# Two-block transformer on one core: the modulation weights with their outputs on partitions, multiplied by VectorE and summed by ScalarE, where TensorE summed them

## The chip, the cores and the metric

One core of one Trainium2 chip runs the whole program. The metric is the device time of one execution in microseconds (us), here the median of three runs.

## The reference

A token array of 512 x 1024 (and later a context of 256 x 1024) goes through two blocks of a first kind (feed-forward, a mixer, feed-forward) and two of a second kind (attention and an MLP). All arithmetic is fp32. Ahead of each of the ten sub-layers stands a modulation: a vector `c` of 1024 numbers is put through silu and multiplied by a 1024 x 3072 matrix, which gives shift, scale and gate for 1024 channels each.

```python
def modulate(x, shift, scale):
    return x * (1.0 + scale) + shift

c_act = jax.nn.silu(c)
for l in range(DEPTH):
    mod = (c_act @ ada_w[l] + ada_b[l]).reshape(b, N_SUB, 3, 1, D_MODEL)
    h = modulate(x, mod[:, 0, 0], mod[:, 0, 1])
    y = swiglu_ffn(h, ffn1_w_in[l], ffn1_w_out[l])
    x = layer_norm(ALPHA * x + 0.5 * mod[:, 0, 2] * y, ln_g[l, 0], ln_b[l, 0])
    ...
```

In the second kind of block there are two such vectors for each matrix, `c_2` for the tokens and `c_ctx_2` for the context. The matrices are numbered m = 0 to 9: m below 6 has one vector, m from 6 on has two. It is this product, vector times matrix, that the change computes in another way. The large matrix products are not touched.

## The kernel before

**The large products.** Each linear layer (`Linear`) is cut into units of weights of up to 128 x 2048. SyncE loads a unit into one of two slots of `raw` (`load_unit`, L893), ScalarE rounds it into `w_hi` (`round_weights`, L1263), VectorE subtracts to get the remainder `w_lo` (`split_weights`, L2760), and TensorE multiplies three times per 128 rows (`passes`, L1935 to L1937): low weights with high data, high with low, high with high. Units alternate between two slots, so unit i is rounded once unit i-2 has been used. In a layer "gateup" (`ffn..._in`) a unit is two tiles of eight chunks, 48 matmuls of 512 columns; ScalarE applies silu to the gate tile (L1299), VectorE multiplies by the other (`val_t`, L2808), ScalarE rounds the result (`hid_hi`, L1305), VectorE takes the remainder (`hid_lo`, L2814). A layer `ffn..._out` has 8 units of one tile each with 12 or 10 chunks. In the MLPs of the second kind of block both streams run: 16 x 3 matmuls of 512 and as many of 256 columns for a unit; ScalarE applies relu (L1340) to each tile.

**The modulation.** Each matrix is cut into 12 units of 128 x 2048 (2 groups of 128 output channels, 8 chunks of 128 inputs; inputs lie on partitions). The first 5 units (`DIRECT`) of m = 0 are multiplied by TensorE, the next 3 (`EARLY`) and all others are spread over the gateup units, one per unit, from the first layer on: 64 units of one vector up to `ffn1_in_1_0`, then 24 units with two vectors in `ffn1_in_1_1`, `ffn2_in_1_0` and the first two units of `ffn2_in_1_1`, then 24 with two vectors over the MLP of the first second-kind block (`number`, `Seg`). Two further slots of `raw` hold these units (`load_ada`, L887). VectorE multiplies a unit by `c` (a number per partition) and adds over the eight chunks: one tensor_scalar and seven scalar_tensor_tensor of 128 x 256 for each vector (`ada_unit`, L2843 and L2846), each waiting for the one before. TensorE then sums the 128 partitions by a matmul with a column of ones:

```python
for q in range(2):
    for v in range(nv):
        mm = eng.matmul(ps[:, B_ADA, at(48 * m + v + (i * 2 + q) * nv)], ada_acc[:, b, v, q * P:(q + 1) * P],
                        ones[:, 0:1], start=True, stop=True, skip_group_check=True)
mm.then_inc(s_asum, 1)
```

**What sets the order.** The order is written out by hand per engine. TensorE's `linear` calls `ada_sums` (L1929) for unit i-2 behind the matmuls of unit i. VectorE's `linear` does, per unit, the remainder of the weights, the evacuation of unit i-2, the modulation unit i-2. ScalarE rounds unit i and evacuates unit i-2. SyncE loads unit i of the layer and modulation unit i-1, the latter once unit i-3 has been multiplied (`s_ada`). `finish` closes a layer: for its last two units it rounds and splits the first two of the following layer, evacuates and, on VectorE, does the modulation unit. At the end, `vectors_of` (before each norm) reads all sums of a matrix.

Of the kernel before, what the change touches and what calls it, by code (L numbers as in the profile page):

```python
# [67 lines left out]
class Seg:  # L68


    def __init__(self, lo, hi, m, u0, a0, p0):
        self.lo, self.hi, self.m, self.u0, self.a0, self.p0 = lo, hi, m, u0, a0, p0
# [81 lines left out]
def ada_parts(m):  # L154

    return DC * vectors(m) - 1


def number(sched):
# [3 lines left out]
    parts = len(EARLY) * ada_parts(0)  # L163
# [29 lines left out]
    for item in sched:  # L193
        if item[0] in ("norm", "ctx_in"):
            item[1].asum = ada
            assert item[1].m is None or m > item[1].m, item[1].name
        if item[0] == "lin":
# [3 lines left out]
            while lo < ln.n and m < 10 and (ln.evac == "gateup" or ln.name == "ffn1_out_0_0" if m < 8 else  # L201
                                            ln.name.startswith("mlp")):
                hi = min(ln.n, lo + ADA_UNITS - u0)
                ln.ada.append(Seg(lo, hi, m, u0, ada, parts))
                u0, ada, parts = u0 + hi - lo, ada + hi - lo, parts + (hi - lo) * ada_parts(m)
# [3 lines left out]
            ln.asum = ada  # L209
# [70 lines left out]
def build(nc, t_in, out):  # L280
# [4 lines left out]
    with ExitStack() as ctx:  # L285
        arena_bytes = 212800
        arena = ctx.enter_context(nc.sbuf_tensor("arena", [P, arena_bytes // 4], F32))
        base = 16512
# [44 lines left out]
        kept = place("kept", [P, 2 * MOD], F32, arena_bytes - 8 * MOD)  # L333
# [12 lines left out]
        assert after("ada_acc") <= used["kept"][0] and after("relu_t") <= after("val_t")  # L346
# [33 lines left out]
        a_head = place("a_head", [P, SSD_H], F32, after("logf"))  # L380
        cacc = place("cacc", [P, 4, SEQ], F32, used["raw"][0] + 2 * 4 * SLOT)
# [186 lines left out]
        s_part = sem("ada_partial_products")  # L568
        s_ada = sem("ada_unit_used")
        s_asum = sem("ada_unit_summed")  # L570
        s_keep = sem("ada_sums_kept")
# [190 lines left out]
        KEPT = {"gqa": 7, "mla": 9}  # L762
# [111 lines left out]
        def _(eng):  # L874
# [22 lines left out]
            for j, item in enumerate(sched):  # L897
                if item[0] == "start":
# [93 lines left out]
        def _(eng):  # L992
# [244 lines left out]
        def _(eng):  # L1237
# [96 lines left out]

            def rectified(ln, i, pos, q):
# [2634 lines left out]
```

## Time and profile before

| | us |
|---|---|
| median of 3 runs (3991.22 to 3994.91) | 3994.83 |
| the profiled execution | 3987.11 |
| its span on the chip | 3985.3 |
| TensorE busy | 3856.9 (97%) |
| VectorE busy | 2538.5 (64%) |
| ScalarE busy | 1385.0 (35%) |
| mean granted TensorE clock | 0.983 of full speed |

PE is TensorE's matmuls, PEld its weight loads (they run beside the matmuls), DVE is VectorE, ACT ScalarE, POOL GpSimd, SP SyncE. A line number is that of the kernel before. A timeline row gives start, duration, engine, line, operation, what is written and read, and how often; in brackets stands how long the engine had been idle and who released it. The profiled execution's time and its span lie 1.8 us apart.

### The profile page before, as it was taken

The numbers are of one execution on the slowest core, as the hardware profiler recorded it, in microseconds if no ns is written. First come the engines' busy times: TensorE is split into PE (matmuls) and PEld (weight loads), VectorE is DVE, ScalarE is ACT, GpSimd is POOL, SyncE is SP. The second block draws the span as 40 slices with busy tenths as digits, with TensorE's granted clock in tenths as the row PEclk, the third lists the DMA queues.
The fourth block names the chain that finished last, engine by engine and source line by source line (L and its number), as shares of the span: only waits on it lengthen the run. The fifth ranks groups of instructions, "written<-read, shape, count | busy, mean of one in ns | idle before, by whom it ended". The sixth has DMA issues, their size and how long they took to land.

```text
span 3985.3 us, 52107 instructions
## 1 busy us (share of the span) xinstructions
PE 3856.9 (97%) x20570; PEld 3256.3 (82%) x20570; DVE 2538.5 (64%) x4095; ACT 1385.0 (35%) x1994; POOL 562.0 (14%) x559
## 2 busy tenths in 40 slices
PE   8999999999999999999998989899999999999998
PEld 6888877888888888788887678888888887888886
DVE  5666776755674677778445489686665367866335
ACT  2222334322232224432222168531221235853223
POOL 1000402200120012130004200150000152113001
PEclk8999999999999999999999989999999999999999
DMA  4554212344343432125322011213322112322221
GB/s 193 192 210 160 84 64 74 138 147 169 138 151 134 178 108 75 43 99 197 127 80 86 11 26 31 74 63 127 127 106 106 59 48 63 70 78 85 95 95 64
DMA packets 71231, 416.00 MB, mean 104 GB/s; under 512 B 8928, under 2 KB 12128, under 8 KB 30048
## 3 DMA queue, kind: packets, MB, share of 16 engines
q1 hardware_dynamic: 69744, 406.63, 29.0%
q10 hardware_dynamic: 1264, 6.29, 0.4%
q8 instruction: 153, 2.51, 0.3%
q14 instruction: 70, 0.57, 0.0%
HBM read 391.92 MB, written 2.10 MB: 99 GB/s over the span
## 4 chain that ended last, share of the span: by engine, by line
PE 82%; DVE 13%; ACT 2%; issue 2%; POOL 2%; DMA 0%; DVEq 0%; ACTq 0%; POOLq 0%
PE ps L1935 25%; PE ps L1936 24%; PE ps L1937 24%; DVE nmax L3726 2%; PE ps L1929 1%; PE ps L2654 1%; DVE w_lo L2760 1%; POOL sq_h_lat L1057 1%; DVE gp_lo L3743 1%; DVE x_lat L3086 1%; DVE rstd_lat L3075 1%; DVE mp_lo L3743 1%; DVE gprob L3738 1%; DVE x_lat L3097 1%; PE ps L2183 1%
## 5 line engine op out<-in xcount | busy, mean ns | idle before, releaser
L1935 PE MATMUL ps<-h_hi,w_lo 128*128 128x512 f32 (+2 forms) x2872 | 1089.9, 379 | 39.8 <-DVE h_lo L3105 17.9
L1937 PE MATMUL ps<-h_hi,w_hi 128*128 128x512 f32 (+2 forms) x2872 | 1069.3, 372 | 0.0
L1936 PE MATMUL ps<-h_lo,w_hi 128*128 128x512 f32 (+1 forms) x2800 | 1043.2, 373 | 0.0
L1263 ACT ACTIVATE w_hi<-raw 128x2048 fp32r<-128x2048 f32 (+3 forms) x262 | 457.8, 1748 | 1368.6 <-PE ps L1937 1326.0
L2760 DVE TENSOR_TENSOR w_lo<-raw,w_hi 128x2048 fp32r<-128x2048 f32 (+3 forms) x262 | 557.9, 2130 | 575.8 <-ACT w_hi L1263 575.5
L1935 PEld LDWEIGHTS ps<-h_hi,w_lo 128*128 128x128 f32 (+1 forms) x2872 | 545.3, 190 | 145.4 <-DVE h_lo L3105 22.5
L1937 PEld LDWEIGHTS ps<-h_hi,w_hi 128*128 128x128 f32 (+1 forms) x2872 | 545.1, 190 | 95.9
L1936 PEld LDWEIGHTS ps<-h_lo,w_hi 128*128 128x128 f32 x2800 | 531.8, 190 | 86.7 <-issue 0.5
L2846 DVE SCALAR_TENSOR_TENSOR ada_acc<-raw,c_act,ada_acc 128x256 f32<-128x256 f32 x1141 | 499.9, 482 | 16.8
L1935 PE MATMUL ps<-hid_hi,w_lo 128*128 128x512 f32 (+1 forms) x1272 | 499.2, 392 | 8.6 <-DVE w_lo L2760 6.5
L1937 PE MATMUL ps<-hid_hi,w_hi 128*128 128x512 f32 (+1 forms) x1272 | 490.4, 386 | 0.0
L1936 PE MATMUL ps<-hid_lo,w_hi 128*128 128x512 f32 (+1 forms) x1272 | 490.2, 385 | 0.0
L1935 PEld LDWEIGHTS ps<-hid_hi,w_lo 128*128 128x128 f32 x1272 | 240.2, 189 | 62.7 <-DVE w_lo L2760 8.8
L1937 PEld LDWEIGHTS ps<-hid_hi,w_hi 128*128 128x128 f32 x1272 | 240.0, 189 | 51.9
L1936 PEld LDWEIGHTS ps<-hid_lo,w_hi 128*128 128x128 f32 x1272 | 240.3, 189 | 50.4 <-issue 1.2
L1028 POOL TENSOR_TENSOR x_sum_lat<-x_lat 128x512 f32<-128x512 f32 x10 | 14.1, 1411 | 1866.6 <-DVE x_lat L3152 1319.8
L3152 DVE SCALAR_TENSOR_TENSOR x_lat<-ps,mod_lat,x_lat 128x512 f32<-128x512 f32 x70 | 52.5, 750 | 183.9 <-PE ps L1937 178.1
L1057 POOL TENSOR_SCALAR sq_h_lat<-x_lat,mod_lat 128x256 f32<-128x256 f32 x144 | 133.6, 935 | 168.3 <-DVE x_lat L3097 168.3
L3726 DVE TENSOR_REDUCE nmax<-ps 128x1 f32<-128x768 f32 x160 | 134.7, 843 | 7.5 <-PE ps L1937 5.6
L1305 ACT ACTIVATE hid_hi<-val_t 128x512 f32 (+1 forms) x88 | 55.6, 632 | 224.7 <-DVE val_t L2808 224.7
L1935 PE MATMUL ps<-hc_hi,w_lo 128*128 128x256 f32 x424 | 122.3, 289 | 8.3 <-DVE hc_lo L3105 8.3
L1441 ACT ACTIVATE h_hi<-x_lat,mod_lat 128x256 fp32r<-128x256 f32 x144 | 79.8, 595 | 125.6 <-DVE x_lat L3097 125.6
(488 smaller groups left out, 6054.1 us busy)
## 6 DMA issues: line engine op xcount, KB each, us to landing
raw<-ada SPq DMA_DIRECT2D x114, 1024.0 KB, 4.9
raw<-ffn_in SPq DMA_DIRECT2D x87, 1024.0 KB, 6.7
raw<-mlp_in SPq DMA_DIRECT2D x32, 1024.0 KB, 4.9
raw<-mlp_out SPq DMA_DIRECT2D x32, 1024.0 KB, 5.1
raw<-ffn_out SPq DMA_DIRECT2D x32, 768.0 KB, 5.4
raw<-ffn_out SPq DMA_DIRECT2D x32, 640.0 KB, 4.0
raw<-mix_p SPq DMA_DIRECT2D x14, 1024.0 KB, 4.8
raw<-mix_x SPq DMA_DIRECT2D x8, 1024.0 KB, 4.9
```

Source lines behind the costliest of these rows:

```text
L1057: eng.tensor_scalar(h32[:, k, part.cs], x[:, k, part.cs], g[:, k:k + 1], b[:, k:k + 1], ALU.mult, ALU.add).then_inc(s_n32, 1)
L1263: eng.activation(w_hi[:, slot, 0:ln.width], raw[:, slot, 0:ln.width], ACT.Copy).then_inc(s_whi, 1)
L1305: eng.activation(hid_hi[:, at(i), :], val_t[:, pos % 2, 0:SEQ].unsqueeze(1), ACT.Copy)\
L1441: eng.activation(hi[:, k, part.cs], x[:, k, part.cs], ACT.Identity, bias=b[:, k:k + 1], scale=g[:, k:k + 1]).then_inc(s_nhi, 1)
L1935: eng.matmul(out, lo_w, hi_x, start=first, stop=False, skip_group_check=True)
L1936: eng.matmul(out, hi_w, lo_x, start=False, stop=False, skip_group_check=True)
L1937: return eng.matmul(out, hi_w, hi_x, start=False, stop=last, skip_group_check=True)
L2760: eng.tensor_tensor(w_lo[:, slot, 0:ln.width], raw[:, slot, 0:ln.width], w_hi[:, slot, 0:ln.width].bitcast(F32), ALU.subtract).then_inc(s_ ...
L2846: ins = eng.scalar_tensor_tensor(acc, weights[:, :, k, :], c_act[:, c:c + 1], acc, ALU.mult, ALU.add)
L3152: a = eng.scalar_tensor_tensor(x, ps[:, tile_bank(ln, m, st), 0:NT[st]], MODT[st][:, ln.gate[st], 2 * DC + m:2 * DC + m + 1], x, ALU.mult, ...
L3726: eng.reduce_max(nmax[:, k % 8:k % 8 + 1], flat(2 * (k % 2))[:, 0:nk], AX_X, negate=True).then_inc(t_mx, 1)
L3743: eng.tensor_tensor(a.p[1][:, k % NPT, :], ps[:, B_PT + k % 2, :], a.p[0][:, k % NPT, :].bitcast(F32), ALU.subtract).then_inc(t_pl, 1)
```

## The change

The modulation weights of all but the first eight units are laid out the other way round: a partition now holds one output channel with its 1024 inputs in a row. VectorE multiplies a whole unit (128 x 2048) by the activated vector, which is laid out along the row and is the same on all partitions (`c_row`, two tensors of 1024 numbers): one tensor_tensor per vector in place of eight instructions. ScalarE runs a Copy over each half of the product (128 x 1024) with its accumulating output, which gives the sum of a row: two activations per vector. TensorE keeps the sums of the three `EARLY` units only, with VectorE's old code for them (`early_unit`, `early_sums`).

Where a product goes:

```diff
+        def product_of(seg, pos, v):
+            if in_place(seg.m, v):
+                return raw[:, 2 + (seg.a0 - seg.lo + pos) % 2, :]
+            if seg.m >= 8:
+                return products2[:, :]
+            return products[:, (seg.s0 + (pos - seg.lo) * vectors(seg.m) + v) % 2, :]
```

On SyncE's queue: the rows of `c`, and a further wait for m = 8 and 9.

```diff
+                    eng.dma_start(c_row[:, 0, :], t_in["c_rows"][0, :].partition_broadcast(P)).then_inc(s_crow, 16)
...
                             eng.wait_ge(s_ada, i + (seg.a0 - seg.lo - 1))
+                            if seg.m >= 8:
+                                eng.wait_ge(s_asum, i * 2 + (seg.s0 - 2 * seg.lo - 2))
...
+                            if ln is rows_ln and i == 4:
+                                eng.wait_ge(s_ada, first_pair.a0)
+                                for v in range(2):
+                                    eng.dma_start(c_row[:, v, :], t_in["c_rows"][1 + v, :].partition_broadcast(P))\
+                                       .then_inc(s_crow, 16)
```

On ScalarE: the sums, one unit behind the evacuation, and at a layer's end.

```diff
+            def ada_sums(seg, i, pos):
+                if seg:
+                    nv, u = vectors(seg.m), seg.u0 - seg.lo
+                    for v in range(nv):
+                        if v + 1 < nv:
+                            eng.wait_ge(s_prod, i + (seg.a0 - seg.lo - first_pair.a0 + 1))
+                        else:
+                            eng.wait_ge(s_ada, i + (seg.a0 - seg.lo + 1))
+                        for q in range(2):
+                            p = product_of(seg, pos, v)[:, q * D:(q + 1) * D]
+                            a = eng.activation(p, p, ACT.Copy, accum_out=sums_of(seg.m)[:, at(i * 2 * nv + (2 * u + q) * nv + v)])
+                        a.then_inc(s_asum, 1)
...
                         round_weights(ln, i, it, lo + u)
                         evacuate(ln, i - 2, it, lo + u - 2)
+                        ada_sums(seg, i - 3, lo + u - 3)
                 finish(ln, lag, following)
...
                     if not first:
                         evacuate(ln, i, 0, i)
+                    if i:
+                        ada_sums_of(ln, i - 1)
                 if following:
                     ahead(following, lag, 2)
+                ada_sums_of(ln, ln.n - 1)
```

On TensorE: the call for the sums goes.

```diff
-                            main(lo + u, i)
-                            if ln.g0 == 0 and lo + u == 7:
-                                eng.wait_ge(s_late, 1)
-                            ada(seg, lo + u - 2, i - 2)
+                    for it, u, i in steps(eng, done, ln.n):
+                        main(done + u, i)
```

On VectorE: a product for each vector.

```diff
+            def ada(seg, i, it, pos):
+                if seg:
+                    nv, n = vectors(seg.m), seg.a0 - seg.lo + pos
+                    raw_ready(eng, 2 + n % 2, n, it)
+                    weights = raw[:, 2 + n % 2, :].rearrange("p (q k) -> p q k", q=2)
+                    eng.wait_ge(s_silu, nv)
                     for v in range(nv):
+                        if not in_place(seg.m, v) and seg.s0 + (pos - seg.lo) * nv + v >= 2:
+                            eng.wait_ge(s_asum, i * nv + (seg.s0 - seg.lo * nv + v - 1))
+                        ins = eng.tensor_tensor(product_of(seg, pos, v).rearrange("p (q k) -> p q k", q=2), weights,
+                                                c_row[:, v, :].unsqueeze(1).broadcast_to([P, 2, D]), ALU.mult)
+                        ins.then_inc(s_prod if v + 1 < nv else s_ada, 1)
```

A product has its own place: two buffers of 128 x 2048 in the space of the context for m below 8, one (`products2`) for the first vector and the slot of `raw` itself for the second (`in_place`) for m = 8 and 9. So VectorE waits, before it writes a product buffer, until ScalarE has summed what was in it, and SyncE, for m = 8 and 9, until the product in the slot is summed. ScalarE activates the rows of `c` itself (`c_rows`: once in the first layer, once at the end of `ffn1_out_1_0`). The sums lie in SBUF (`ada_sum`, `kept`) and no longer in a PSUM bank, so the two copies `keep` and the waits for them go. To find the room the region for DMA descriptors is cut from 16 to 8 KiB per partition.

TensorE's queue in a gateup layer (names: `h_hi`, `h_lo` the data, `w_hi`, `w_lo` the weights, `ada_acc` the partial sums). Before, at a unit's end:

```order
L1936 MATMUL ps<-h_lo,w_hi 128x512
L1937 MATMUL ps<-h_hi,w_hi 128x512
L1929 MATMUL ps<-ones,ada_acc 128x1 x2
L1935 MATMUL ps<-h_hi,w_lo 128x512
L1936 MATMUL ps<-h_lo,w_hi 128x512
```

After the change the two matmuls on `ada_acc` are gone and nothing stands in their place.

ScalarE's queue at the end of `ffn1_in_1_1`, the layer with two vectors per unit, where `ffn1_out_1_1` (units of 128 x 1280) begins. Before:

```order
L1263 ACTIVATE w_hi<-raw 128x1280
L1299 ACTIVATE gate_t<-ps 128x512
L1305 ACTIVATE hid_hi<-val_t 128x512
L1263 ACTIVATE w_hi<-raw 128x1280
L1299 ACTIVATE gate_t<-ps 128x512
L1305 ACTIVATE hid_hi<-val_t 128x512
L1263 ACTIVATE w_hi<-raw 128x1280 x5
```

After the change:

```order
L1296 ACTIVATE w_hi<-raw 128x1280
L1332 ACTIVATE gate_t<-ps 128x512
L1338 ACTIVATE hid_hi<-val_t 128x512
L1379 ACTIVATE products,ada_sum<-products 128x1024 x4
L1296 ACTIVATE w_hi<-raw 128x1280
L1332 ACTIVATE gate_t<-ps 128x512
L1338 ACTIVATE hid_hi<-val_t 128x512
L1379 ACTIVATE products,ada_sum<-products 128x1024 x8
L1296 ACTIVATE w_hi<-raw 128x1280 x5
```

Eight sums, those of the last two units, now stand ahead of the rounding of the third unit of the following layer (the first of the x5).

VectorE's queue at the same place. Before:

```order
L2760 TENSOR_TENSOR w_lo<-raw,w_hi 128x1280
L2808 TENSOR_TENSOR val_t<-ps,gate_t 128x512
L2814 TENSOR_TENSOR hid_lo<-val_t,hid_hi 128x512
L2843 TENSOR_SCALAR ada_acc<-raw,c_act 128x256 x2
L2846 SCALAR_TENSOR_TENSOR ada_acc<-raw,c_act,ada_acc 128x256 x14
L3152 SCALAR_TENSOR_TENSOR x_lat<-ps,mod_lat,x_lat 128x512
L2760 TENSOR_TENSOR w_lo<-raw,w_hi 128x1280
```

After the change:

```order
L2803 TENSOR_TENSOR w_lo<-raw,w_hi 128x1280
L2851 TENSOR_TENSOR val_t<-ps,gate_t 128x512
L2857 TENSOR_TENSOR hid_lo<-val_t,hid_hi 128x512
L2899 TENSOR_TENSOR products<-raw,c_row 128x2048 x2
L3196 SCALAR_TENSOR_TENSOR x_lat<-ps,mod_lat,x_lat 128x512
L2803 TENSOR_TENSOR w_lo<-raw,w_hi 128x1280
```

Two products stand where sixteen small instructions stood; the rest has kept its place.

## Rows read from the trace of the kernel before

**Rows 1.** The page: busy time, shares of the chain, a transfer (us to landing last).
```profile
PE 3856.9 (97%) x20570; PEld 3256.3 (82%) x20570; DVE 2538.5 (64%) x4095; ACT 1385.0 (35%) x1994; POOL 562.0 (14%) x559
...
PE 82%; DVE 13%; ACT 2%; issue 2%; POOL 2%; DMA 0%; DVEq 0%; ACTq 0%; POOLq 0%
...
raw<-ffn_in SPq DMA_DIRECT2D x87, 1024.0 KB, 6.7
```

**Rows 2.** Groups by line and shape: busy us, mean ns of one | idle before.
```profile
L2760 DVE TENSOR_TENSOR w_lo<-raw,w_hi 128x2048 fp32r<-128x2048 f32 x187 | 431.4, 2308 | 408.5 <-ACT w_hi L1263 408.3
L1929 PE MATMUL ps<-ones,ada_acc 128*128 128x1 f32 x652 | 79.3, 236 | 0.0
L1411 ACT ACTIVATE sq_h_lat<-x_lat 128x1024 f32<-128x1024 f32 x18 | 19.1, 1061 | 19.3 <-DVE x_lat L3025 18.9
L1817 ACT ACTIVATION_READ_ACCUMULATOR gprob<-ps,nmax 128x1 f32 x96 | 18.7, 195 | 0.0
```

**Rows 3.** Timeline of ACT, rounding: one vector, two vectors, no modulation units.
```profile
118.76 1.92 ACT L1263 ACTIVATE w_hi<-raw 128x2048 fp32r<-128x2048 f32 x1 [5.84 <-PE ps L1937]
130.11 1.92 ACT L1263 ACTIVATE w_hi<-raw 128x2048 fp32r<-128x2048 f32 x1 [5.84 <-PE ps L1937]
...
1352.59 1.92 ACT L1263 ACTIVATE w_hi<-raw 128x2048 fp32r<-128x2048 f32 x1 [6.28 <-PE ps L1937]
1364.40 1.92 ACT L1263 ACTIVATE w_hi<-raw 128x2048 fp32r<-128x2048 f32 x1 [6.21 <-PE ps L1937]
...
2057.87 1.92 ACT L1263 ACTIVATE w_hi<-raw 128x2048 fp32r<-128x2048 f32 x1 [5.37 <-PE ps L1937]
2068.75 1.27 ACT L1263 ACTIVATE w_hi<-raw 128x1280 fp32r<-128x1280 f32 x1 [5.37 <-PE ps L1937]
```

**Rows 4.** Timeline of PE at a unit's end in the MLP with both streams.
```profile
3084.02 0.29 PE L1937 MATMUL ps<-hc_hi,w_hi 128*128 128x256 f32 x1
...
3084.95 0.48 PE L1935 MATMUL ps<-h_hi,w_lo 128*128 128x512 f32 x1
...
3085.50 0.39 PE L1937 MATMUL ps<-h_hi,w_hi 128*128 128x512 f32 x1
```

**Rows 5.** Timelines of DVE, PE and POOL at the beginning of `ffn2_in_1_0`.
```profile
1782.95 1.04 DVE L2814 TENSOR_TENSOR hid_lo<-val_t,hid_hi 128x512 fp32r<-128x512 f32 x1
1784.76 6.05 DVE L2846 SCALAR_TENSOR_TENSOR ada_acc<-raw,c_act,ada_acc 128x256 f32<-128x256 f32 x14
...
1793.76 0.47 PE L1935 MATMUL ps<-h_hi,w_lo 128*128 128x512 f32 x1 [0.97 <-DVE val_t L2808]
...
1774.53 12.45 POOL L1069 TENSOR_SCALAR x_lat<-x_lat,aff_lat 128x256 f32<-128x256 f32 x16
```

**Rows 6.** Timeline of ACT where an exponential with accumulating output is followed by another.
```profile
2324.84 0.90 ACT L1817 ACTIVATE gprob<-ps,nmax 128x768 f32<-128x768 f32 x1 [1.39 <-DVE nmax L3726]
...
2325.73 0.89 ACT L1817 ACTIVATE gprob<-ps,nmax 128x768 f32<-128x768 f32 x1
```

**Rows 7.** Timeline of ACT at the end of `ffn1_in_1_1` and of `ffn2_in_1_0`.
```profile
1423.31 1.27 ACT L1263 ACTIVATE w_hi<-raw 128x1280 fp32r<-128x1280 f32 x1 [7.74 <-PE ps L1937]
...
1426.74 0.63 ACT L1305 ACTIVATE hid_hi<-val_t 128x512 fp32r<-128x512 f32 x1 [1.67 <-DVE val_t L2808]
1431.17 1.27 ACT L1263 ACTIVATE w_hi<-raw 128x1280 fp32r<-128x1280 f32 x1 [3.80 <-PE ps L1937]
...
1899.34 1.49 ACT L1263 ACTIVATE w_hi<-raw 128x1536 fp32r<-128x1536 f32 x1 [7.26 <-PE ps L1937]
...
1903.25 0.63 ACT L1305 ACTIVATE hid_hi<-val_t 128x512 fp32r<-128x512 f32 x1 [1.94 <-DVE val_t L2808]
1908.61 1.49 ACT L1263 ACTIVATE w_hi<-raw 128x1536 fp32r<-128x1536 f32 x1 [4.72 <-PE ps L1937]
```

**Rows 8.** Timeline of ACT in an MLP unit with both streams and no modulation.
```profile
3111.17 0.87 ACT L1340 ACTIVATE relu_t<-ps 128x512 f32<-128x512 f32 x2 [5.74 <-PE ps L1937]
...
3127.89 0.87 ACT L1340 ACTIVATE relu_t<-ps 128x512 f32<-128x512 f32 x2 [4.86 <-PE ps L1937]
```

More of the change, by code:

```diff
@@ L151, in vectors, with in_place @@
     return 1 if m < 6 else 2
-def ada_parts(m):
-    return DC * vectors(m) - 1
+def in_place(m, v):
+    return m >= 8 and v == 1
 def number(sched):
@@ L162, in number @@
     ada = len(EARLY)
-    parts = len(EARLY) * ada_parts(0)
+    sums = 0
     m, u0 = 0, len(DIRECT) + len(EARLY)
@@ L332, in build @@
         hc_lo = place("hc_lo", [P, DC, CTX], F32R, after("hc_hi"))
-        kept = place("kept", [P, 2 * MOD], F32, arena_bytes - 8 * MOD)
+        c_row = place("c_row", [P, 2, D], F32, arena_bytes - 8 * D)
+        kept = place("kept", [P, 2 * MOD], F32, arena_bytes - 8 * D - 8 * MOD)
+        ada_sum = place("ada_sum", [P, 4, 2 * MOD], F32, used["kept"][0] - 32 * 32)
+        products = place("products", [P, 2, SLOT], F32, used["hc_hi"][0])
         A = after("hc_lo")
@@ L345, in build @@
         ada_acc = place("ada_acc", [P, 2, 2, 2 * P], F32, after("val_t"))
-        assert after("ada_acc") <= used["kept"][0] and after("relu_t") <= after("val_t")
+        products2 = place("products2", [P, SLOT], F32, after("relu_t"))
+        assert after("ada_acc") <= used["ada_sum"][0] and after("relu_t") <= after("val_t")
+        assert after("products2") <= used["ada_sum"][0] and after("products") <= A and after("ada_sum") <= used["kept"][0]
         sq_a = {"lat": place("sq_a_lat", [P, DC, SEQ], F32, A)}
@@ L864, in weight_half, with sums_of @@
             return slice(h * ln.width // 2, (h + 1) * ln.width // 2)
+        first_pair = next(seg for item in sched if item[0] == "lin" for seg in item[1].ada if vectors(seg.m) == 2)
+        rows_ln = next(item[1] for item in sched if item[0] == "lin" and any(seg is first_pair for seg in item[1].ada))
+        rows_ln = sched[next(j for j, item in enumerate(sched) if item[1] is rows_ln) - 1][1]
+        assert rows_ln.n == DC and not rows_ln.ada and not first_pair.lo and not first_pair.u0
+        def sums_of(m):
+            return kept[:, :] if m in (7, 9) else ada_sum[:, m % 4, :]
+        def product_of(seg, pos, v):
[4 more added lines that the diff above has]
+            return products[:, (seg.s0 + (pos - seg.lo) * vectors(seg.m) + v) % 2, :]
         def raw_ready(eng, slot, n, it):
@@ L1333, in evacuate, with ada_sums_of, c_rows @@
                         a.then_inc(s_hidhi, 1)
+            def ada_sums(seg, i, pos):
[10 more added lines that the diff above has]
+                        a.then_inc(s_asum, 1)
+            def ada_sums_of(ln, i):
+                for lo, hi, seg in runs(ln, 0, i, i + 1):
+                    ada_sums(seg, i, i)
+            def c_rows(n):
+                eng.wait_ge(s_crow, 16 if n == 0 else 48)
+                c = c_row[:, 0, :] if n == 0 else c_row[:, :, :]
+                eng.activation(c, c, ACT.Silu).then_inc(s_silu, 1)
             def rectified(ln, i, pos, q):
@@ L1375, in linear @@
                     third_unit(ln)
-                for lo, hi, _ in runs(ln, 2, lag + (ln.halved is not None), ln.n):
+                if ln.g0 == 0:
+                    c_rows(0)
+                for lo, hi, seg in runs(ln, 3, lag + (ln.halved is not None), ln.n):
                     for it, u, i in steps(eng, lo, hi):
@@ L2150, in linear @@
                     return
-                if before and before.ada:
-                    ada_of(before, before.n - 2)
-                    if ln.n > 1:
-                        main(1, 1)
-                        done = 2
-                    ada_of(before, before.n - 1)
                 if ln.norm:
@@ L3532, in mixer @@
                 w.h_chunks += DC
-            def keep(kind):
-                m = KEPT[kind]
-                eng.wait_ge(s_asum, ADA_UNITS * (m + 1) - len(DIRECT))
-                eng.tensor_copy(kept[:, :], ps[:, B_ADA, 48 * m:48 * m + 2 * MOD]).then_inc(s_keep, 1)
             def split_keys(v):
```

134 lines of the change are left out of this document (61 added, 73 removed).

## The prediction, made before the change was run

> **What bounds the kernel.** I read the page first: TensorE is busy 97% of the span, VectorE 64%, ScalarE 35%, and the chain of work that ended last lies on TensorE for 82% [rows 1]. So a microsecond of TensorE's queue is worth a microsecond of the whole, and one of VectorE or ScalarE nothing, as long as they hand their results over in time. Then I read the groups by line and shape for what the sums cost TensorE, and the timelines for how long a unit takes with and without them. The group [rows 2] has 652 records of L1929 (each fp32 matmul leaves two), 79.3 us in all; but matmuls overlap, so the time that they take from the queue is read from the distance of unit to unit. ScalarE rounds the next unit as soon as TensorE has ended one, which makes its rounding a clock for TensorE's progress: 130.11 - 118.76 = 11.35 us with one vector, 1364.40 - 1352.59 = 11.81 with two, 2068.75 - 2057.87 = 10.88 where no modulation unit is left [rows 3]. 10.88 is 48 matmuls at 0.227 with nothing between, so a unit's end costs nothing by itself and the sums are the whole difference.
>
> **TensorE: what goes.** With one vector 11.35 - 10.88 = 0.47 us per unit, 64 units: 30.1. With two vectors in the gateup layers 0.93, 24 units: 22.3. In the MLP with both streams I take TensorE's own rows: from the last matmul before the sums to the third after them 3085.50 - 3084.02 = 1.48 us [rows 4]. Without sums it would be one of 256 columns and two of 512; a unit there takes 3127.89 - 3111.17 = 16.72 for 48 of each [rows 8], so 0.12 for the one and 0.57 for the three. That leaves 0.91, 24 units: 21.8. Together **74.2 us**. The three EARLY units keep their sums. The waits and copies for the kept sums cost TensorE nothing I can see, and I take nothing for them.
>
> **VectorE: what goes.** A unit's eight or sixteen small instructions become one or two products of 128 x 2048 with both inputs in SBUF. The row nearest in shape and kind is the remainder of the weights, 2.31 us [rows 2], and I take 2.3. Two vectors: 4.6 in place of over 6 (14 of the 16 alone took 6.05 in [rows 5]). TensorE rarely waits for this: at the beginning of `ffn2_in_1_0` the sixteen stand ahead of the fourth unit's remainder, and TensorE idles 0.97 before it goes on [rows 5]. The products end over a microsecond sooner, so I count **1.0 us** gained. The next thing late there is ScalarE's rounding, which is long done. The remaining gain on VectorE is worth nothing: it lies beside TensorE's matmuls.
>
> At this place GpSimd runs until 1786.98 (12.45 from 1774.53), and VectorE's remainder took 1.04 there [rows 5], where other instructions of its kind take about 0.7. So a product that begins there is stretched, by my estimate 0.5 to 1 us over the pair, and it still ends in time. The Trainium skill speaks against the change here (SBUF — State Buffer, "Who interferes with whom"): a VectorE instruction with two SBUF inputs contends with a GpSimd instruction that reads SBUF, and whoever issues first holds the shared pair for its whole duration. Taken as a full block, the first product would wait out GpSimd's last 3 us, the 1.0 would not be gained, and the sum would come out about 1 us higher.
>
> **ScalarE: what comes.** 2 activations per vector and unit, 64 x 2 + 48 x 4 = 320, each with a read of the accumulator. A square of the same 128 x 1024 takes 1.06, the read 0.195 [rows 2]; one after the other without overlap 1.25. But in the row of exponentials the next one starts 2325.73 - 2324.84 = 0.89 after the one before, read included, though the activation alone lasts 0.90 [rows 6]: the read hides in the overlap. So I take **1.05 per sum**, with 1.25 as the upper end; the lower end of their cost to TensorE is nothing. That is 336 us more on ScalarE, 1385 to about 1720, 43% of the span.
>
> Do they hide? In a gateup unit with one vector ScalarE gets 2.1 us more in 10.88, behind its evacuation. With two vectors there is a ring: VectorE may write a product only when ScalarE has summed the one before in that buffer. That ring is: four sums 4.2, the last product 2.3, then the remainder, `val_t` and `hid_hi` before ScalarE can sum again: the rounding to the end of `hid_hi` is 1427.37 - 1423.31 = 4.06 with narrow weights [rows 7], of which 1.27 is the rounding; the remainder of the full width adds 0.9, so 3.7. The ring is 10.2, under 10.88 (with 1.25 per sum 11.0, level with it). And TensorE needs the split weights only at the end of the unit, 10.88 - 1.92 - 2.31 = 6.7 us after they are there. SyncE's load of the next gateup unit stands behind its wait for the product, which ends some 1.5 us into the following unit; landing takes 6.7 [rows 1], before the 10.88 are over. In the MLP a unit's first product ends about 8.4 us after its odd tile (relu 0.87, rounding 1.92, remainder 2.31, the hidden tile's remainder about 1, product 2.3), the four sums at 12.6; the relu of the next tile, due at 8.4, must be through with its square by 16.7 [rows 8]: 12.6 + 0.9 + 1.0 = 14.5, so it hides.
>
> They don't hide at a layer's end. There eight sums stand ahead of the third rounding of the following layer. In `ffn1_out_1_1`, with the rounding at 1423.31 as zero: `hid_hi` ends at 4.06, the sums of the last unit but one at 8.3; the last unit's products, each waiting for a buffer, end at 8.5 and 10.8, their sums at 10.6 and 12.9; rounding 1.27 gives 14.2, the remainder (1280 of 2048 columns of 2.31, 1.4) 15.6. TensorE has done two units of 1431.17 - 1423.31 - 0.93 = 6.93, 13.9 [rows 7]: **1.7 us lost**. The same for `ffn2_out_1_0`: `hid_hi` at 4.54, sums at 13.4, rounded 14.9, split 16.6, against 2 x (9.27 - 0.93) = 16.7: nothing. With 1.25 per sum the two lose 2.9 and 1.1, 4.0. With one vector four sums end before 10, and nothing is lost.
>
> Edits with no cost: the first row of `c` (512 KB) is loaded while TensorE is at the opening's own sums, its silu (about 1.1 us of ScalarE, by the square's row) stands ahead of the fourth rounding, on a queue that is idle most of the time there; the other two rows load and activate in `ffn1_out_1_0`, where no modulation unit is due. If that cover were gone it would be 1 to 2 us each, once. The smaller descriptor region I cost at nothing: its price shows in no row.
>
> **The sum.** -74.2 - 1.0 + 1.7 = **-73.5 us**. The profiled execution, 3987.1 (span 3985.3 and 1.8 around it), becomes 3913.6. The median of the runs lies 7.7 above the profiled execution; I take the same difference from it: 3994.8 - 73.5 = **3921**.
>
> **Rivals.**
> (a) *ScalarE's sums are dearer, 1.3 to 1.6 us, and the ring fills.* At 1.5: the ring is 12.0, 1.1 over for 24 units, of which the 6.7 of slack in each of three stretches swallow all but some 6; the two ends lose 5.3 and 3.5. Loss 15 in place of 1.7: 3934. For it: the upper bound of 1.25 is near, and sums written through a register address show in no row. Against: the overlap of [rows 6].
> (b) *The accumulating Copy costs twice a plain one, and ScalarE's ring becomes the bound.* It decides from about 1.9 us per sum: the ring is 13.6, 2.7 over, 65 less 20 of slack is 45; in the 12 `mlp_in` units the relu comes 4 x 1.9 - 6.3 = 1.3 late, 16; the ends lose 8 x 0.85 more each, 15: 76, all that was gained. At 2.12 (two squares) it is 65 + 26 + 19 = 110, 35 more than is gained: 4030. For it: one ring holds both engines and the product's buffers. Against: the exponentials with accumulator cost no more than their width.
> (c) *The change doesn't free TensorE*: something else fills the places of the sums, time 3995. Against: [rows 3], where units without sums follow at full rate.
>
> **How the numbers follow.** Forecast 0.80; (a) 0.11; (b) 0.05; (c) 0.04. 0.2% of the time is 8 us, about what runs can tell from no change. Faster by more: 0.91; within it 0.04; slower 0.05. Range: low end 3910, where no sum is paid for, other short waits for VectorE shrink with its load, and the runs' own scatter of 4 us is added; high end 3940, which takes in 1.25 per sum and all of (a).
>
> **What would show it.** Right: ScalarE's roundings 10.88 apart in all gateup stages; TensorE's 652 records on `ada_acc` down to 12; ScalarE near 1720 us busy, VectorE some 170 us less; 320 sums 1.05 apart; one new wait of TensorE of 1 to 3 us near the beginning of `ffn1_out_1_1`. Wrong: periods over 10.88 with two vectors and ScalarE never idle in them (a, b); idle TensorE at each unit's end (c); waits of ScalarE for transfers that reach TensorE.

## The result, and the profile after

The changed kernel takes **3922.8 us** (median of 4 runs, 3916.2 to 3930.5) against 3993.0 (4 runs, 3989.6 to 3994.9) of the kernel before: 70.2 us less, ratio 0.983 with a 95% interval of 0.982 to 0.985. The forecast was 3921, and 73.5 less. The profiled execution is the longest of the four, 3930.5 (span 3928.7, granted clock 0.980), so its distance to the profiled execution of before, 56.7, is not the gain; where most of the other 14 us went is told below.

Line numbers are now those of the changed kernel: rounding L1296, split L2803, sum L1379, product L2899, the three passes L2000 to L2002, a hidden chunk's split L2857 and L2968, evacuation into `x_lat` L2870 and L3196. First its page:

```profile
PE 3793.1 (97%) x19930; PEld 3189.2 (81%) x19930; DVE 2365.4 (60%) x2973; ACT 1724.5 (44%) x2636; POOL 575.9 (15%) x559
```

Against [rows 1], TensorE has 640 records fewer (12 of the 652 are left), VectorE is 173 us less busy, ScalarE 340 more. The groups by line and shape give the prices of the new instructions:

```profile
L2899 DVE TENSOR_TENSOR products<-raw,c_row 128x2048 f32<-128x2048 f32 x136 | 309.3, 2289 | 27.7 <-ACT products L1379 27.7
L1379 ACT ACTIVATE products<-products 128x1024 f32<-128x1024 f32 x272 | 284.2, 1048 | 119.3 <-DVE products L2899 119.3
L1379 ACT ACTIVATION_READ_ACCUMULATOR products<-products 128x1 f32 x240 | 44.2, 184 | 0.0
```

A product takes 2.29 us, a sum 1.05, its read 0.18. In the timeline of ScalarE, a one-vector stretch and a two-vector unit, the answer to [rows 3]:

```profile
126.00 1.92 ACT L1296 ACTIVATE w_hi<-raw 128x2048 fp32r<-128x2048 f32 x1 [3.29 <-PE ps L2002]
136.88 1.92 ACT L1296 ACTIVATE w_hi<-raw 128x2048 fp32r<-128x2048 f32 x1 [3.29 <-PE ps L2002]
...
1331.22 1.92 ACT L1296 ACTIVATE w_hi<-raw 128x2048 fp32r<-128x2048 f32 x1 [1.21 <-PE ps L2002]
1336.63 1.04 ACT L1379 ACTIVATE products<-products 128x1024 f32<-128x1024 f32 x1
1337.67 1.05 ACT L1379 ACTIVATE products<-products 128x1024 f32<-128x1024 f32 x1
...
1342.10 1.92 ACT L1296 ACTIVATE w_hi<-raw 128x2048 fp32r<-128x2048 f32 x1 [1.21 <-PE ps L2002]
```

The roundings stand 10.88 apart with one vector and with two; sums follow each other in 1.04 (the read hides, as in [rows 6]); and ahead of each rounding ScalarE is still idle for 1.21 with two vectors. VectorE too waits for that rounding:

```profile
1344.05 2.29 DVE L2803 TENSOR_TENSOR w_lo<-raw,w_hi 128x2048 fp32r<-128x2048 f32 x1 [0.72 <-ACT w_hi L1296]
```

So the ring, which runs over VectorE's products, could close 0.72 us sooner than it does: it is not full. The waits of TensorE by releaser, of the kernel after:

```profile
PE ps L2000 <- DVE w_lo L2803: 17.9, 8, 5.9
...
PE ps L2000 <- DVE hidc_lo L2968: 4.5, 4, 1.1
...
PE ps L2000 <- DVE x_lat L2870: 0.8, 1, 0.8
```

and of the kernel before:

```profile
PE ps L1935 <- DVE w_lo L2760: 16.0, 6, 5.9
...
PE ps L1935 <- DVE hidc_lo L2922: 1.9, 4, 1.1
PE ps L1935 <- DVE val_t L2808: 1.0, 1, 1.0
```

The wait of 1.0 for `val_t` is gone [rows 5]. New are 1.9 more for `w_lo` (1.8 of it at one place), 0.8 for `x_lat` at one place, and 2.6 more for the hidden chunks at three. The first is the end of `ffn1_in_1_1`, here in the timelines of ScalarE, VectorE and TensorE:

```profile
1396.50 1.28 ACT L1296 ACTIVATE w_hi<-raw 128x1280 fp32r<-128x1280 f32 x1 [2.65 <-PE ps L2002]
...
1400.47 1.05 ACT L1379 ACTIVATE products<-products 128x1024 f32<-128x1024 f32 x1
...
1408.36 1.04 ACT L1379 ACTIVATE products<-products 128x1024 f32<-128x1024 f32 x1
1409.40 2.42 ACT L1296 ACTIVATE w_hi<-raw 128x1280 fp32r<-128x1280 f32 x2
...
1410.68 1.49 DVE L2803 TENSOR_TENSOR w_lo<-raw,w_hi 128x1280 fp32r<-128x1280 f32 x1 [2.76 <-ACT w_hi L1296]
...
1410.06 0.40 PE L2002 MATMUL ps<-hid_hi,w_hi 128*128 128x512 f32 x1
1412.23 0.50 PE L2000 MATMUL ps<-hid_hi,w_lo 128*128 128x512 f32 x1 [1.77 <-DVE w_lo L2803]
```

With the rounding at 1396.50 as zero, the eight sums end and the third rounding begins at 12.9, and the split is done at 15.7: the forecast's numbers to 0.1. From matmul to matmul TensorE takes 2.17 in place of 0.23, so **1.95 us** are lost. The second is the end of `ffn2_in_1_0`, VectorE and TensorE:

```profile
1879.19 1.76 DVE L2803 TENSOR_TENSOR w_lo<-raw,w_hi 128x1536 fp32r<-128x1536 f32 x1 [3.73 <-ACT w_hi L1296]
1880.87 0.74 DVE L2870 SCALAR_TENSOR_TENSOR x_lat<-ps,mod_lat,x_lat 128x512 f32<-128x512 f32 x1
...
1880.57 0.40 PE L2002 MATMUL ps<-hid_hi,w_hi 128*128 128x512 f32 x1
1881.76 0.47 PE L2000 MATMUL ps<-hid_hi,w_lo 128*128 128x512 f32 x1 [0.80 <-DVE x_lat L2870]
```

The split is there with the last matmul of the second unit, as forecast, but TensorE waits for the bank of the first tile, and its evacuation stands *behind* the split on VectorE: **0.97 us** lost. The third place is the handover from `mlp_in` to `mlp_out`, on TensorE, which comes four times:

```profile
2810.89 0.40 PE L2002 MATMUL ps<-hid_hi,w_hi 128*128 128x512 f32 x1
2812.42 0.51 PE L2000 MATMUL ps<-hid_hi,w_lo 128*128 128x512 f32 x1 [1.13 <-DVE hidc_lo L2968]
```

Here it takes 1.53 in place of 0.23, 1.30 lost at each. Before, it was 0.44 at three of the four, and 1.30 at the last, where no modulation unit was due any more:

```profile
2716.52 0.40 PE L1937 MATMUL ps<-hid_hi,w_hi 128*128 128x512 f32 x1
2717.18 0.50 PE L1935 MATMUL ps<-hid_hi,w_lo 128*128 128x512 f32 x1 [0.26 <-DVE hidc_lo L2922]
```

The tally: -74.2 - 1.0 + 1.95 + 0.97 + 3 x 0.87 = **-69.7**, against -70.2 between the medians. That they agree to half a microsecond is luck, for the interval of the ratio is 11 us wide. And the traces give the sums a little less than 74.2. Both have the same 19918 records of matmuls besides the sums' own, so each can be laid beside its counterpart ("aligned" here and below). Over the places of the sums the changed kernel gains 29.6, 21.9 and 21.3 us, together 72.8: a unit with two vectors gave 0.92 in a gateup layer but 0.88 at an output layer and in the MLP.

**The profiled execution's missing 14 us.** Aligned with it, the changed kernel is 7.7 us behind before at 106 us (8.3 at 80), and the work there is the same. The windows of the opening show why, first the kernel before, then the kernel after:

```profile
0.00:50.00 50.00, 44.25 (x198) 34.95 (x199) 26.07 (x33) 12.96 (x13) 6.22 (x21) 0.80 0.71 282
50.00:100.00 50.00, 41.86 (x173) 34.07 (x172) 24.54 (x52) 13.13 (x15) 10.10 (x13) 0.89 0.27 102
```
```profile
0.00:50.00 50.00, 44.31 (x174) 33.49 (x174) 26.06 (x33) 12.91 (x13) 6.22 (x21) 0.75 0.66 269
50.00:100.00 50.00, 41.87 (x159) 34.50 (x160) 17.81 (x35) 12.20 (x14) 10.10 (x13) 0.78 0.25 89
```

The number ahead of the last two is the granted clock: 0.80 and 0.89 against 0.75 and 0.78. The trace holds 30.7 us at the lower level (1.2 GHz) before 100 us in the one, 47.8 in the other. The experiments' profiles show that this goes with the run and not with the change. From 106 us on the two profiles differ by 64.4, some 4 less than the terms add up to (72.8 + 1.0 less the 5.5 of the three places): 1.5 are a stretch of 3.4 us at the lower level at 1666.4 us, which the other profiles don't have there, and the rest, between 2100 and 3600 us, I did not follow.

### The profile page after: what moved, and what is told of

It reads as the page before. It is cut to its first block, busy times and chain, and to the rows that moved or that the text cites. A ratio compares the mean times of both kernels' runs of the same rounds, so it can differ in the third digit from the quotient of the medians.

```text
span 3928.7 us, 49772 instructions
## 1 busy us (share of the span) xinstructions
PE 3793.1 (97%) x19930; PEld 3189.2 (81%) x19930; DVE 2365.4 (60%) x2973; ACT 1724.5 (44%) x2636; POOL 575.9 (15%) x559
## 4 chain that ended last, share of the span: by engine, by line
PE 81%; DVE 13%; ACT 2%; issue 2%; POOL 2%; DMA 0%; DVEq 0%; ACTq 0%; POOLq 0%
PE ps L2000 25%; PE ps L2001 24%; PE ps L2002 24%; DVE nmax L3762 2%; DVE w_lo L2803 1%; PE ps L2697 1%; DVE gp_lo L3779 1%; POOL sq_h_lat L1090 1%; DVE x_lat L3130 1%; DVE rstd_lat L3119 1%; PE ps L2228 1%; DVE mp_lo L3779 1%; DVE gprob L3774 1%; DVE x_lat L3141 1%; DVE h_lo L3149 1%
## 5 line engine op out<-in xcount | busy, mean ns | idle before, releaser
L2000 PE MATMUL ps<-h_hi,w_lo 128*128 128x512 f32 (+2 forms) x2872 | 1085.7, 378 | 40.9 <-DVE h_lo L3149 19.4
L2002 PE MATMUL ps<-h_hi,w_hi 128*128 128x512 f32 (+2 forms) x2872 | 1071.1, 373 | 0.0
L2803 DVE TENSOR_TENSOR w_lo<-raw,w_hi 128x2048 fp32r<-128x2048 f32 (+3 forms) x262 | 558.2, 2131 | 657.6 <-ACT w_hi L1296 657.3
L1296 ACT ACTIVATE w_hi<-raw 128x2048 fp32r<-128x2048 f32 (+3 forms) x262 | 457.6, 1747 | 972.3 <-PE ps L2002 961.5
L2000 PEld LDWEIGHTS ps<-h_hi,w_lo 128*128 128x128 f32 (+1 forms) x2872 | 546.7, 190 | 148.5 <-DVE h_lo L3149 23.3
L2002 PEld LDWEIGHTS ps<-h_hi,w_hi 128*128 128x128 f32 (+1 forms) x2872 | 546.6, 190 | 95.3
L2000 PE MATMUL ps<-hid_hi,w_lo 128*128 128x512 f32 (+1 forms) x1272 | 496.3, 390 | 13.8 <-DVE w_lo L2803 8.5
L2002 PE MATMUL ps<-hid_hi,w_hi 128*128 128x512 f32 (+1 forms) x1272 | 490.4, 386 | 0.0
L1379 ACT ACTIVATE products<-products 128x1024 f32<-128x1024 f32 x272 | 284.2, 1048 | 119.3 <-DVE products L2899 119.3
L2899 DVE TENSOR_TENSOR products<-raw,c_row 128x2048 f32<-128x2048 f32 x136 | 309.3, 2289 | 27.7 <-ACT products L1379 27.7
L2000 PEld LDWEIGHTS ps<-hid_hi,w_lo 128*128 128x128 f32 x1272 | 239.7, 188 | 70.5 <-DVE w_lo L2803 12.3
L2002 PEld LDWEIGHTS ps<-hid_hi,w_hi 128*128 128x128 f32 x1272 | 239.7, 188 | 52.4
L3196 DVE SCALAR_TENSOR_TENSOR x_lat<-ps,mod_lat,x_lat 128x512 f32<-128x512 f32 x70 | 52.4, 749 | 177.3 <-PE ps L2002 171.4
L1338 ACT ACTIVATE hid_hi<-val_t 128x512 fp32r<-128x512 f32 (+1 forms) x88 | 55.6, 632 | 212.1 <-DVE val_t L2851 212.1
```

What stands on the lines that cost most here:

```text
L1296: eng.activation(w_hi[:, slot, 0:ln.width], raw[:, slot, 0:ln.width], ACT.Copy).then_inc(s_whi, 1)
L1338: eng.activation(hid_hi[:, at(i), :], val_t[:, pos % 2, 0:SEQ].unsqueeze(1), ACT.Copy)\
L1379: a = eng.activation(p, p, ACT.Copy, accum_out=sums_of(seg.m)[:, at(i * 2 * nv + (2 * u + q) * nv + v)])
L2000: eng.matmul(out, lo_w, hi_x, start=first, stop=False, skip_group_check=True)
L2002: return eng.matmul(out, hi_w, hi_x, start=False, stop=last, skip_group_check=True)
L2803: eng.tensor_tensor(w_lo[:, slot, 0:ln.width], raw[:, slot, 0:ln.width], w_hi[:, slot, 0:ln.width].bitcast(F32), ALU.subtract).then_inc(s_ ...
```

## The experiments

The first four ran beside 15 runs of the kernel before (median 3995.6), the last three beside 15 more (3995.1), all on one chip. Run 1 is the changed kernel, against which the others are read.

**1. The change again.** No edit.

> The changed kernel once more, unaltered, as the measure for the three runs beside it. Expected: 69 to 71 us under the kernel before (0.982 to 0.983 of it). Its first four runs lay between 3916 and 3930 us with granted clocks of 0.983 to 0.980, so single runs should again differ by some 10 us and go with the granted clock; if the profiled run has a clock of 0.983, its opening should be as long as the opening before. If instead the opening of the changed kernel is slower in itself (its matmul groups of 16 at 7 us against 9.6 us in the two profiles), some 8 us should be lost in the first 80 us in this profile too.

3925.0 (3918.7 to 3930.0, 5 runs), ratio 0.982 (0.981 to 0.984): 70.5 us less. The profiled run lost 3.9 us in the opening, with 41.0 us at the lower level. Both new waits are at their places with the same 1.95 and 0.97. Directly behind the first, which ends at 1408.7 here, the clock falls for 3.4 us (from 1410.0), which the first profile did not have.

**2. ScalarE's last sums behind the rounding.**

```diff
+                if ln.ada and following and following.n > 2 and len(following.streams) == 1:
+                    w.held = ln
+                else:
+                    ada_sums_of(ln, ln.n - 1)
...
                     round_weights(ln, i, 0, i)
+                    held_sums()
...
+                    if ln.evac == "resid" and ln.n > 2 and ln.halved is None:
+                        evacuate(ln, done - 2, 0, done - 2)
+                        split_weights(ln, done, 0, done)
```

> The changed kernel with two edits at the end of a layer: ScalarE takes the sums of the layer's last unit behind the third rounding of the layer that follows (not ahead of it), and in the output layers without a norm VectorE evacuates the first tile ahead of the third split. My reading of the trace after (new waits of 1.95 us near 1410 and 0.97 us near 1881 on TensorE) says that both waits go and nothing takes their place: 2.9 us under the changed kernel. The rival reading, that these waits belong to a late transfer or a bank and not to the eight sums, leaves both where they are: 0. Total difference is below the scatter of single runs, so the two places in the trace decide.

3920.1 (3916.5 to 3925.3, 5 runs), 0.982 (0.981 to 0.983), 4.9 under run 1, within its scatter. The places decide. ScalarE's timeline, with four sums where there were eight:

```profile
1388.67 1.28 ACT L1298 ACTIVATE w_hi<-raw 128x1280 fp32r<-128x1280 f32 x1 [2.64 <-PE ps L2022]
1396.80 1.26 ACT L1298 ACTIVATE w_hi<-raw 128x1280 fp32r<-128x1280 f32 x1
1402.66 1.27 ACT L1298 ACTIVATE w_hi<-raw 128x1280 fp32r<-128x1280 f32 x1 [0.44 <-PE ps L2022]
```

The third rounding (1396.80) begins 8.1 us after the second in place of 12.9, TensorE's waits for `w_lo` are back to 16.2, and the one for `x_lat` L2870 is gone. Aligned with run 1, the kernel gains 3.6 us at the first place (1.95, and the rest is the 3.4 us at half clock that followed it) and 1.0 at the second, and nothing is lost between. Both waits belong to the order on the two engines: the first to the sums ahead of the rounding, the second to the split ahead of the evacuation.

**3. TensorE's matmuls put back.**

```diff
+                def idle(seg):
+                    if seg:
+                        for j in range(2 * vectors(seg.m)):
+                            eng.matmul(ps[:, B_ADA, j:j + 1], ones[:, :], ones[:, 0:1], start=True, stop=True,
+                                       skip_group_check=True)
```

> The changed kernel, with ScalarE and VectorE as they are, but TensorE gets its fp32 matmuls of one column back at the old places: two per unit with one vector, four per unit with two, on constants, into an unused bank, and nobody waits for them. If TensorE's own time is the whole gain (64 x 0.47 + 24 x 0.93 + 24 x 0.91 = 74.2 us, of which some 2.6 us stand in the cover of the hidden chunks' last chain), the time goes back to the kernel before within 4 us: about 3990 to 3994 (0.999 to 1.000 of it). If part of the gain came from VectorE's lighter work or from waits between the engines, it stays under the kernel before by that part: 3960 to 3985.

3990.1 (3986.7 to 3996.3, 11 runs), 0.9994 (0.9985 to 1.0003). The gain is gone, as it should be. A group by line, the roundings of ScalarE with two vectors, and TensorE's waits for the hidden chunk:

```profile
L2201 PE MATMUL ps<-ones 128*128 128x1 f32 x640 | 77.4, 235 | 0.0
```
```profile
1350.59 1.92 ACT L1296 ACTIVATE w_hi<-raw 128x2048 fp32r<-128x2048 f32 x1 [1.21 <-PE ps L2002]
1362.41 1.92 ACT L1296 ACTIVATE w_hi<-raw 128x2048 fp32r<-128x2048 f32 x1 [2.15 <-PE ps L2002]
```
```profile
PE ps L2000 <- DVE hidc_lo L2987: 1.9, 4, 1.1
```

The period is 11.82 again [rows 3], and the handovers are back to 1.9 us in all. Aligned with the kernel before matmul by matmul, this run stands 9.1 us behind it at 510 us (all of it from the opening, 47.8 us at the lower level), 10.1 at 1763, 9.1 at 1814, where the wait for `val_t` was, and 9.3 at 2065. So, with ScalarE's 340 us more and VectorE's 171 less, and TensorE as before, the two kernels run level but for that 1.05 us. In the MLP, from 2700 to 3100, their distance stays within 0.1, and at the end it is 8.7. VectorE's relief is worth 1 us and no more. The median is 5.4 us under that of the kernel before, which is within the scatter: the interval of the ratio holds 1.

**4. Short sums.** `p = product_of(seg, pos, v)[:, q * D:q * D + 8]`.

> The changed kernel with each of ScalarE's sums over 8 columns in place of 1024 (the other 1016 are left out of the modulation's sums), so that a sum costs some 0.25 us in place of 1.04 and ScalarE does some 250 us less. If ScalarE's load is hidden as I took it, only the two waits at layer ends go: about 2.9 us under the changed kernel, at most 4. If the sums cost more than that, by filled rings or by traffic on SBUF that slows the other engines' work, the time falls by 8 us or more.

3917.7 (3914.4 to 3919.9, 5 runs), 0.981 (0.980 to 0.982), 7.3 under run 1: between the two expectations. Aligned with run 2, which has the full sums, it settles: between 106 and 2008 us, the whole of the gateup layers with sums, the distance of the two changes by no more than 0.13 us at any matmul, but for 4 us near 637 where the clock changed, and in the MLP, from 2640 to 3100, by 0.02. ScalarE has 270 us less to do (1454.2 busy) and TensorE does not notice. The profile of run 1 is 10.8 us longer than this one: 4.2 by the opening's clock (41.0 us at the lower level against 30.7), 3.6 at the first new wait and 1.0 at the second, as in run 2, and the rest behind 2008 us, where the two profiles' clocks fall at other places.

**5 and 6. ScalarE loaded.** Ahead of each gateup sum stands a copy on constants (the third line of the edit has its columns):

```diff
+                            r = (seg.s0 + (pos - seg.lo) * nv + v) % 2 * 2 + q
+                            if seg.m < 8:
+                                for lo, hi in ((0, 512),):
+                                    eng.activation(extra[:, r, lo:hi] if r < 3 else ps[:, B_ADA, lo:hi], par[:, lo:hi],
+                                                   ACT.Copy)
```

Run 6 has `((0, 416), (416, 448), (448, 480), (480, 512))` in the third line.

> The changed kernel, and in the gateup layers each of ScalarE's 224 sums (64 units of two, 24 units of four) has a plain copy of 512 columns ahead of it, on constants, some 0.56 us each by the rows of such copies. By my ring (between two roundings of weights stand one unit's evacuations and its sums: 4 sums + 5.9 us against TensorE's 10.88 us per unit) the ring of the two-vector units becomes 4 x 1.6 + 5.9 = 12.3 us: 1.4 us over, in 9 units of each of two layers, less the 6.7 us by which a rounding stands ahead of its use: 12 us; and at the ends of layers eight (four) sums ahead of the third rounding cost some 13 us. Sum: 25 us over the changed kernel (18 to 32). One-vector units (2 x 1.6 + 5.9 = 9.1 us) lose nothing inside a layer. If ScalarE has much more slack than that, under 8 us; if every us of ScalarE's counts, 125 us.

> As the run beside it, but with a copy of 416 columns and three of 32 ahead of each sum, together some 1.15 us, so that a sum costs about 2.2 us: the price of my second rival. By my ring: 4 x 2.2 + 5.9 = 14.7 us, 3.8 us over TensorE's 10.88, in 9 units of two layers, less 6.7 each: 55 us; ends of the two-vector layers 2 x 9.2, of five one-vector layers some 2.6 each: 31 us. Sum: 86 us over the changed kernel (70 to 100), that is slower than the kernel before. If the ring has more slack than I read, under 40 us; if every us of ScalarE's counts, 258 us.

Run 5: 3955.9 (3953.1 to 3959.1, 4 runs), 0.991 (0.989 to 0.992), 31 over run 1. Run 6: 3982.7 (3980.1 to 3992.6, 10 runs), 0.998 (0.997 to 0.999), 58 over run 1, where 86 (70 to 100) was expected: a miss. The roundings of runs 5 and 6:

```profile
1361.05 1.91 ACT L1297 ACTIVATE w_hi<-raw 128x2048 fp32r<-128x2048 f32 x1
1373.09 1.90 ACT L1297 ACTIVATE w_hi<-raw 128x2048 fp32r<-128x2048 f32 x1
```
```profile
1360.25 0.89 ACT L1383 ACTIVATE extra<-par 128x416 f32<-128x416 f32 x4
1361.05 1.04 ACT L1385 ACTIVATE products<-products 128x1024 f32<-128x1024 f32 x1
...
1367.61 1.90 ACT L1297 ACTIVATE w_hi<-raw 128x2048 fp32r<-128x2048 f32 x1
1380.76 1.90 ACT L1297 ACTIVATE w_hi<-raw 128x2048 fp32r<-128x2048 f32 x1
```

ScalarE is idle ahead of none of them: the ring is full. Its period is 12.04 in run 5 (12.3 expected). In run 6 the four copies came to 0.80 us in place of 1.15, since small ones overlap: 4 x 1.84 + 5.9 = 13.3, measured 13.15. So the period of the full ring holds to 0.3 us, and the price put into it was too high: 4 x 0.36 us per unit in 18 units is 26 of the 28 us by which run 6 came out lower. The layers' ends were mis-sized too. TensorE's waits in run 5:

```profile
PE ps L2006 <- DVE w_lo L2809: 21.2, 8, 5.9
PE ps L2006 <- DVE hid_lo L2863: 11.0, 2, 6.1
PE ps L2006 <- DVE val_t L2857: 7.7, 9, 1.0
```

The filled ring inside the layers is the last line, 7.7 us. At each of the two ends TensorE first waits 5 to 6 us for the last hidden chunk, which stands behind the sums, and then 5.0 for the third unit's weights at the one end and 4.2 for the bank of the first tile (`x_lat`) at the other. By the steps from matmul to matmul these four waits lose 20.9 us, where run 1 loses 2.9. With each came a stretch of 6.8 us at the lower level, which begins 0.6 to 3.4 us before the wait ends; the matmuls behind the waits lose 9.7 us by it in all, where run 1 loses 1.7. So run 5's 31 us lie in the expected range in part by luck, for they are made up otherwise than I had written. The profiles of runs 5 and 1 differ by 33.2 us: some 11 in the ring, where I had 12, 18 in the waits at the ends, where I had 13, and 8 by the clock, which I did not have, less 4.6 by which run 5's opening is shorter. The windows 1400 to 1420 of runs 5, 1 and 2 (TensorE busy, its clock):

```profile
1400.00:1420.00 20.00, 12.79 (x41) 0.76 0.23 68
```
```profile
1400.00:1420.00 20.00, 18.23 (x72) 0.91 0.21 66
```
```profile
1400.00:1420.00 20.00, 20.00 (x88) 1.00 0.29 99
```

One-vector layers lost nothing in run 5 and 0.6 us in run 6, where I had put 13 for them.

**7. The version that beats both.** Run 2 and, in `both_streams`, on ScalarE and with `split_hidden` on VectorE:

```diff
-                    elif following and i - ln.n < following.n:
+                    elif following and i - ln.n < following.n and not (relu and i > ln.n):
                         ahead(following, i - ln.n, i - ln.n + 1)
                     if relu:
                         hidden(ln, i - 2, 1)
+                    if relu and i > ln.n and following and following.n > 1:
+                        ahead(following, 1, 2)
```

> The changed kernel with the two edits of the run with the last sums behind the rounding, and a third: at the end of the MLP's first layer the rounding and split of the next layer's second unit stand behind the rounding and split of the last hidden chunk, not ahead of them. My reading is that the four new waits of 1.30 us (0.44 before) at the handover of the two MLP layers come from that chunk's chain (6.1 us from the tile's end to its split, 1.9 and 2.3 us of it the other unit's rounding and split): 4 x 1.3 = 5.2 us more, 8.1 us under the changed kernel with the 2.9 us of the other two edits, ratio 0.980 to 0.981. If that chain is set by something else, the waits stay and the time is that of the run with the two edits.

3916.4 (3910.9 to 3917.0, 5 runs), ratio 0.9806 (0.979 to 0.982): 78.6 under the kernel before and 8.6 under run 1 by the medians (8.1 expected); the intervals of the two ratios overlap, so the places carry the proof. TensorE's waits have no line for a hidden chunk any more; at each of the four handovers the step is 0.24 in place of 1.53, and aligned with run 2 it gains 1.4 us at each. The chain was the other unit's rounding and split, as read.

## Why the prediction was right, and where it was not

- **TensorE, -74.2:** right in the gateup layers to 1 us. Each period came out at the forecast's 10.88, and run 3 gave all of it back; but in the units of the output layers behind them the pair cost 0.44 and the four 0.88, not 0.47 and 0.93. In the MLP 21.8 was too much by 0.5, at 0.88 or 0.89 a unit in place of 0.91, and by 2.6 more: I took 24 times 0.91 as lost time, but at three layer ends the matmuls of the sums stood in the cover of the last hidden chunk's chain, that is, in time in which TensorE would have waited for it anyway. The kernel before showed this: its fourth handover, where no sums stand, has the 1.30 already. I had read it as a place without modulation and not compared it with the other three.
- **VectorE, -1.0:** right, 1.05 in run 3. The product pair beside GpSimd took 4.76, 0.27 over its 4.49 elsewhere; I had said 0.5 to 1.
- **ScalarE's sums at 1.05, hidden inside the layers:** right. 1.04 from start to start, 1724.5 busy against 1720; run 4, which takes 270 of the 340 us away, shows that they cost nothing there. The ring: 10.88 less the 0.72 that VectorE idles is 10.2, as forecast. ScalarE's own queue has another count: 9.67 from a rounding to the end of the last sum (2.48 of them idle, for `val_t`) and 1.21 idle.
- **Layer ends, +1.7:** `ffn1_out_1_1` right (1.95). `ffn2_out_1_0` wrong, 0.97 in place of nothing: I followed the chain to the split and stopped there, though VectorE still had the tile to evacuate behind it, and TensorE waits for that bank too. Run 2 takes both away.
- **The sum:** -73.5 forecast, -70 measured. The missed terms are 1.4 (the sums' steps), 0.97, 0.25 and 2.6, all the same way: 5.2, which makes -68.3. They are small, and so the middle of the range held. That 3922.8 lies only 1.8 from 3921 is in part luck: the runs beside it put the kernel before at 3993.0 and not 3994.8, and the medians' distance is 2 us over what the places add up to.
- **Rivals.** (a) and (b) needed dearer sums, and these cost 1.04. Their periods would have shown in the roundings, as runs 5 and 6 do, where ScalarE is never idle ahead of one. (b)'s threshold can be checked: at 1.84 us per sum, in the gateup layers alone, run 6 is still 12 us faster than the kernel before, and (b) put the break-even at 1.9 with the MLP's share in it. Its terms were distributed otherwise: less in the ring, more at the two ends, where I had one late item and there are two, and the clock adds to it. Whether the whole would cross at 1.9 was not tried in the MLP. (c) fell with the periods.

## What to carry to other kernels

Work moved from the engine that bounds to one that has room is worth its distance from start to start on the first, less what of it stood in time in which that engine would have waited for another's chain; look at the ends of layers for such waits, and compare an end with the work and one without it. Inside a loop a moved load is free until its ring (the chain from a buffer's use to its next use) is as long as the loop's period; at an end it piles up ahead of the next layer's first items, so follow each wait of the bounding engine there (weights, bank, input chunk), not only the latest you know of. At an end, put first what the bounding engine needs first, and work that nobody waits for last: here the three edits were worth 8 us.

## What the runs showed of the hardware

- **A long stall costs more than itself.** With each of the four stalls of 4 to 6 us in run 5 the granted clock was at 1.2 GHz for 6.8 us: from 1398.8, 1415.8, 1890.3 and 1907.4, where the stalls end at 1402.2, 1416.7, 1892.2 and 1908.0. The matmuls that fell into these stretches stand 0.43 apart in place of 0.23, and cost 1.6, 2.8, 2.3 and 2.9 us more. After the wait of 1.95 us the clock fell in one of the two profiles that have it (3.4 us, 1.7 lost), after the one of 0.97 in neither.
- **The opening's clock goes with the run.** In the opening, whose matmuls are the same in all nine profiles but for one unit's sums, the lower level held for 30.7 us in five of them, 41.0 in one (run 1) and 47.8 in three, worth up to 8 us, which is half of the scatter between runs. Of the 30 runs of the kernel before beside the experiments, those with a mean clock of 0.983 took 3986.5 to 3987.9 us, those with 0.981 3995.1 to 3996.3. So two profiles are compared by place, and totals by medians.
- **GpSimd is stopped by VectorE's products.** At the beginning of `ffn2_in_1_0`, GpSimd's multiplications take 0.55 alone, and beside the two products:

```profile
1757.68 3.10 POOL L1102 TENSOR_SCALAR x_lat<-x_lat,aff_lat 128x256 f32<-128x256 f32 x1
1760.77 4.70 POOL L1102 TENSOR_SCALAR x_lat<-x_lat,aff_lat 128x256 f32<-128x256 f32 x1
```
```profile
1758.16 2.28 DVE L2899 TENSOR_TENSOR products<-raw,c_row 128x2048 f32<-128x2048 f32 x1
1760.36 2.56 DVE L2899 TENSOR_TENSOR products<-raw,c_row 128x2048 f32<-128x2048 f32 x1
1762.84 2.28 DVE L2803 TENSOR_TENSOR w_lo<-raw,w_hi 128x2048 fp32r<-128x2048 f32 x1
```

The first of GpSimd's two lasts until the first product is through, the second through the second product and the split behind it, all with two inputs in SBUF. GpSimd's sixteen now take 17.76 in place of 12.45 [rows 5]. The rule is in the Trainium skill (SBUF — State Buffer, "Who interferes with whom"): a VectorE instruction with two SBUF inputs contends with a GpSimd instruction that reads SBUF, the ports that they share are an exclusive lock, and the order of issue decides who blocks. The trace agrees, 3.10 and 4.70 in place of 0.55. (That a holder keeps them for its whole instruction the section spells out for VectorE's two-port modes; these rows go with it for two SBUF inputs.) I had read the rule as a risk for VectorE, waiting out all of GpSimd's work. The products were not held up so: the first began directly behind the instruction before it and took 2.28, and the second took 0.27 more. My reading is that a holder keeps the lock for one instruction, GpSimd's are 0.55 and VectorE's 2.3, so the one with the long instructions wins; no run tests it. TensorE waited for nobody here, so it cost nothing.
- **Small activations overlap.** In run 6 a copy of 416 columns is 0.54 us long in the rows and one of 32 columns 0.21, so one and three add up to 1.17; but from the start of the first to the start of the sum behind them it is 0.80. The sum of the rows overstates a chain of small activations.
